# A stick-breaking attention stage: sigmoid(-z) goes into the PSUM bank of the scores instead of a ring in SBUF

## Chip, cores, metric

The kernel runs on one core of one Trainium2 chip. The metric is the device time of one execution in microseconds (us).

## The reference

One decoder layer over 1024 tokens of width 1024, all in float32: RMSNorm, one combined projection, a retention group (4 heads of 128), a stick-breaking attention group (8 heads of 64), an output projection, and a top-4-of-32 mixture of experts. The part that the change touches is the stick-breaking group. For each head and each block of 128 queries it computes

```python
z = einsum('bhqd,bhkd->bhqk', q_blk, kt) * scale
causal = key_pos[None, :] < q_pos[:, None]
log_one_minus = where(causal, log_sigmoid(-z), 0.0)
log_remaining = cumsum(log_one_minus, axis=3, reverse=True) - log_one_minus
weights = where(causal, exp(log_sigmoid(z) + log_remaining), 0.0)
out = einsum('bhqk,bhkd->bhqd', weights, vt)
```

So a weight is sigmoid(z) times the product of sigmoid(-z) over all later keys up to the query.

## The kernel before

The kernel is written out by hand for each engine, with semaphores between them; every engine runs its own list in program order. Its stages follow each other: norm and projections with the retention work (to about 403 us of the profiled execution), stick-breaking attention (403 to 566 us), output projection and routing (to about 715 us with the list work), and a loop over 32 experts from there to the end.

The attention stage works in *units*. A unit is one head, one block of 128 queries (i = 0 to 7) and up to 512 keys; a query block with more than 512 keys has two units per head, the later keys first. The two heads of a pair (par 0 and 1) always come together, so the work goes in doubles, units n and n+1 with n even. A pair has 24 units, the four pairs 96 (NU). In order, the 12 doubles of a pair have 128, 256, 384, 512, 128, 512, 256, 512, 384, 512, 512 and 512 columns (the fifth and sixth belong to i = 4, and so on). For a unit n:

- TensorE, scores(n) (L871 to L894, called with even n for both heads): three passes of matmuls of the split queries and keys into bank[n % 4] (L881, L884, L887), and for the block on the diagonal a matmul that adds a mask (L893). It raises z_ok.
- ScalarE, remains(n) (L681): sigmoid(-z) of the bank into `stick`, a ring of four units in SBUF. It raises z_not. sticks(n) (L688): sigmoid(z) of the same bank into `sig`, a ring of six in SBUF. It raises z_sig.
- VectorE, remaining(n) (L1256): a running product (tensor_tensor_scan, L1267) over stick[n % 4] from the last key to the first, into `rem`; its second input is a column of ones, broadcast. It raises z_rem. Where a query block has two units, the second starts from the first one's last value.
- GpSimd (L540 to L544): sig times rem, shifted by one, in place in sig. It raises z_w.
- TensorE, turn_weights(n) (L896): up to four 128x128 transposes into bank 4 or 5 (L901); ScalarE, turned(n) (L694): copy to `wgtT` (L699); TensorE, values(n) (L904): matmuls with the values into bank 6 or 7 (L913).

The order of the lists: TensorE runs values(n - 8), turn_weights(n - 4), turn_weights(n - 3), scores(n + 4) for n in steps of two. ScalarE runs turned(n - 6), turned(n - 5), remains(n), remains(n + 1), sticks(n), sticks(n + 1). VectorE runs remaining(n) for n in turn, and for a pair with another behind it four steps that split the next pair's queries and keys (pair_step, L1193: a cast L1198 or a subtraction L1201 over 1024 columns), behind units 6, 10, 14 and 18 of the pair's 24; a copy of a finished output bank (chain_out, L1273) comes ten units behind its last unit.

A score bank is used again four units later. scores(n) waits for the two sigmoids of unit n - 3 (z_not and z_sig at n - 2), and remains(n) waits for the running product of unit n - 4, since that read the same place of the ring. The stages behind start from z_pv (values of all units) and z_out.

Of the kernel before, what the change touches and what calls it, by code (L numbers as in the profile page):

```python
# [34 lines left out]
ACT = mybir.ActivationFunctionType  # L35
# [11 lines left out]
CH = 512  # L47
# [60 lines left out]
def layer(nc, x, attn_norm_g, w_in, ret_norm_g, sb_q_norm_g, sb_k_norm_g, w_out, ffn_norm_g,  # L108
          w_router, b_router, w_gate_up, b_gate_up, w_down, b_down, consts, rope, out):
    with ExitStack() as ctx:  # L110
# [3 lines left out]
        def sb(name, shape, dt=F32):  # L114
            return ctx.enter_context(nc.sbuf_tensor(name, shape, dt))

        def sem(name):
            return ctx.enter_context(nc.semaphore(name))
# [6 lines left out]
        ring = sb("ring", [P, 24576])  # L125
# [5 lines left out]
        bank = [ctx.enter_context(nc.psum_tensor(f"bank{i}", [P, 512], F32)) for i in range(8)]  # L131
# [17 lines left out]
        def region(t, at, *shape):  # L149
            n = int(np.prod(shape))  # L150
            v = t[:, at:at + n]
            if len(shape) == 1:
                return v
            names = "abcd"[:len(shape)]
            return v.rearrange(f"p ({' '.join(names)}) -> p {' '.join(names)}",
                               **{k: s for k, s in zip(names, shape)})
# [28 lines left out]
        prj_std = region(work, 9216, CH)  # L185
        rem = region(work, 0, 4, D + 2)
        wgtT = region(work, 4104, 4, CH)
        stick = region(ring, 3072, 4, CH)
        sig = region(ring, 5120, 6, CH)
        ident_r = region(ring_r, 128, P)  # L190
        mask_r = region(ring_r, 256, P)
# [77 lines left out]
        z_sig = sem("z_sig")  # L269
        z_not = sem("z_not")  # L270
        z_rem = sem("z_rem")
# [81 lines left out]
        units = []  # L353
        for p in range(SH // 2):
            for i in range(NT):
                for k0 in ((0,) if i < HT else (CH, 0)):
                    k1 = min(k0 + CH, (i + 1) * P)
                    for par in range(2):
                        units.append(dict(p=p, par=par, h=2 * p + par, i=i, k0=k0, n=(k1 - k0) // P, w=k1 - k0,
                                          at=D - (i + 1) * P + k0, row=(2 * (NT * p + i) + par) % 4,  # L360
# [18 lines left out]
        def unit_before(n):  # L379

            u = units[n]
            same = [m for m in range(n) if units[m]["row"] == u["row"] and units[m]["last"]]
            return same[-1] if same else None
# [212 lines left out]
        def _(e):  # L596
# [81 lines left out]
                            e.wait_ge(r_acc, c - 1)  # L678
                        e.activation(k_tok[:, c % 2], bank[4][:, :], ACT.Copy).then_inc(r_k, 1)

            def remains(n):  # L681
                w = units[n]["w"]
                e.wait_ge(z_ok, n + 1)
                if n >= 4:
                    e.wait_ge(z_rem, n - 3)
                e.activation(stick[:, n % 4, 0:w], bank[n % 4][:, 0:w], ACT.Sigmoid, scale=-1.0).then_inc(z_not, 1)  # L686

            def sticks(n):  # L688
                w = units[n]["w"]
                if n >= 6:  # L690
                    e.wait_ge(z_tr, n - 5)
                e.activation(sig[:, n % 6, 0:w], bank[n % 4][:, 0:w], ACT.Sigmoid).then_inc(z_sig, 1)

            def turned(n):  # L694
                w = units[n]["w"]
                e.wait_ge(z_tr, n + 1)
                if n >= 4:
                    e.wait_ge(z_pv, n - 3)
                e.activation(wgtT[:, n % 4, 0:w], bank[4 + n % 2][:, 0:w], ACT.Copy).then_inc(z_wT, 1)  # L699
# [3 lines left out]
            for n in range(0, NU + 6, 2):  # L703
                if n >= 6:
                    turned(n - 6)
                    turned(n - 5)
                if n < NU:
                    for m in (n, n + 1):
                        remains(m)
                    for m in (n, n + 1):  # L710
                        sticks(m)
            e.wait_ge(z_pv, NU)
            for i in range(2):
                e.dma_start(x_re[:, i], xr[i]).then_inc(xr_in[i], 16)
# [54 lines left out]
        def _(e):  # L769
# [101 lines left out]
            def scores(n):  # L871
                u = units[n]
                b, p = u["p"] % 2, u["p"]
                e.wait_ge(z_st, 4 * (p + 1))
                if n >= 4:
                    e.wait_ge(z_not, n - 2)
                    e.wait_ge(z_sig, n - 2)
                queries, keys = slice(u["i"] * P, (u["i"] + 1) * P), slice(u["k0"], u["k0"] + u["w"])
                heads = ((n, slice(0, HD)), (n + 1, slice(HD, P)))
                for m, pr in heads:  # L880
                    e.matmul(bank[m % 4][:, 0:u["w"]], q_hi[b][pr, queries], k_hi[b][pr, keys], start=True, stop=False,  # L881
                             skip_group_check=True)
                for m, pr in heads:
                    e.matmul(bank[m % 4][:, 0:u["w"]], q_hi[b][pr, queries], k_lo[pr, p, keys], start=False, stop=False,  # L884
                             skip_group_check=True)
                for m, pr in heads:
                    mm = e.matmul(bank[m % 4][:, 0:u["w"]], q_lo[pr, p, queries], k_hi[b][pr, keys], start=False,  # L887
                                  stop=not u["diag"], skip_group_check=True)
                    if not u["diag"]:
                        mm.then_inc(z_ok, 1)  # L890
                if u["diag"]:
                    for m, pr in heads:
                        e.matmul(bank[m % 4][:, u["w"] - P:u["w"]], ident_r, mask_r, start=False, stop=True,  # L893
                                 skip_group_check=True).then_inc(z_ok, 1)  # L894
# [28 lines left out]
            for n in range(-4, NU + 8, 2):  # L923
                if n >= 8:
                    values(n - 8)
                if 4 <= n < NU + 4:
                    turn_weights(n - 4)
                    turn_weights(n - 3)
                if n + 4 < NU:
                    scores(n + 4)  # L930
# [53 lines left out]
            for j in range(NT - 1):  # L984
                n = NT - 1 - j
# [124 lines left out]
        def _(e):  # L1110
# [92 lines left out]
            for g, u in enumerate(groups):  # L1203
# [34 lines left out]
                if c == 6:  # L1238
                    e.wait_ge(prj, g + 1)
                    at = SL * (u["slab"] % 2)  # L1240
# [15 lines left out]
            def remaining(n):  # L1256
                u = units[n]
                e.wait_ge(z_not, n + 1)
                if u["diag"]:
                    before_it = unit_before(n)  # L1260
                    if before_it is not None:
                        e.wait_ge(z_w, before_it + 1)
                    left = 1.0
                else:
                    e.wait_ge(z_rem, n - 1)
                    left = rem[:, u["row"], u["at"] + u["w"]:u["at"] + u["w"] + 1]
                e.tensor_tensor_scan(rem[:, u["row"], u["at"]:u["at"] + u["w"]][:, ::-1], stick[:, n % 4, 0:u["w"]][:, ::-1],  # L1267
                                     ones[:, 0:1].to_broadcast([P, u["w"]]), left, ALU.mult, ALU.mult).then_inc(z_rem, 1)

            def chain_out(n):  # L1270
# [7 lines left out]
            for n in range(NU + 10):  # L1278
                if n < NU:
                    remaining(n)  # L1280
                    p, j = n // PAIR + 1, n % PAIR - 6
                    if p < SH // 2 and 0 <= j < 16 and j % 4 == 0:
                        if j == 0 and p >= 2:
                            e.wait_ge(z_ok, PAIR * (p - 1))
                        pair_step(p, j // 4)
                if n >= 10 and units[n - 10]["ends"] and units[n - 10]["par"] == 1:
                    chain_out(n - 10)
# [248 lines left out]
```

## Time and profile before

| | |
|---|---|
| time, median of 3 runs | 2402.2 us (2400.37 to 2408.03) |
| the profiled execution's own time | 2400.01 us |
| its span in the profile | 2398.1 us |
| busy in the span | TensorE 95%, VectorE 41%, ScalarE 21%, GpSimd 15% |
| attention stage | 403 to 566 us |

The profile shows one execution. PE is TensorE (PEld its weight loads), DVE is VectorE, ACT ScalarE, POOL GpSimd; L1267 is line 1267 of the kernel. Busy time says how long an engine had an instruction in it, also while that instruction was held up. What a wait is put down to is the line that released it.

### The profile page before, as it was taken

How to read it: one execution, taken by the hardware profiler on the slowest of the kernel's cores; microseconds unless marked ns; L12 is line 12 of the kernel's file. 1: busy time of each engine (PE TensorE's matmuls, PEld its weight loads, DVE VectorE, ACT ScalarE, POOL GpSimd, SP SyncE). 2: the span in 40 equal slices, each digit the busy share in tenths (PEclk: the TensorE clock that was granted, in tenths of full speed). 3: DMA queues.
4: the chain of work that ended last, by engine and by line, in shares of the span. 5: the costliest groups of instructions: out<-in, count | busy, mean ns of one | idle time of the engine just before them, and what ended most of it. 6: DMA issues, size and time to landing. Idle time of an engine off the chain costs nothing.

```text
span 2398.1 us, 43829 instructions
## 1 busy us (share of the span) xinstructions
PE 2283.4 (95%) x17841; PEld 2167.5 (90%) x17842; DVE 994.9 (41%) x2198; ACT 492.9 (21%) x938; POOL 354.1 (15%) x263
## 2 busy tenths in 40 slices
PE   6999999888969999999999999999999999999997
PEld 5878888566869999999999999999999999999997
DVE  6435435997354333233333333332333333333332
ACT  4243144776111111011111111111111111111110
POOL 1101202894000100010010100010001010101001
PEclk9999999999969999999999999999999999999999
DMA  4222222003357888778888887887888887888882
GB/s 161 97 71 71 91 86 88 1 2 120 127 194 234 257 290 264 227 253 288 282 262 289 274 257 250 283 261 231 278 291 276 285 268 234 261 288 277 288 282 37
DMA packets 250237, 501.97 MB, mean 209 GB/s; under 512 B 7884, under 2 KB 36592, under 8 KB 250112
## 3 DMA queue, kind: packets, MB, share of 16 engines
q1 hardware_dynamic: 233888, 449.87, 53.7%
q0 software_dynamic: 14912, 45.71, 9.5%
q10 hardware_dynamic: 1344, 5.01, 0.7%
q8 instruction: 76, 1.25, 0.2%
q14 instruction: 17, 0.14, 0.0%
HBM read 469.46 MB, written 31.10 MB: 209 GB/s over the span
## 4 chain that ended last, share of the span: by engine, by line
PE 87%; issue 4%; DVE 3%; POOL 3%; ACT 1%; DMA 1%; DVEq 0%; ACTq 0%; POOLq 0%
PE bank L1045 43%; PE bank L1056 19%; PE bank L799 13%; POOL ring L544 3%; PE bank L1033 2%; DVE hx L1408 2%; PE bank L1004 2%; PE bank L948 1%; PE bank L950 1%; PE bank L949 1%; PE bank L996 1%; PE bank L901 1%; PE bank L807 1%; PE bank L913 0%; PE bank L969 0%
## 5 line engine op out<-in xcount | busy, mean ns | idle before, releaser
L1045 PE MATMUL bank<-hx,ring 128*128 128x140 f32 (+1 forms) x8192 | 1034.9, 288 | 25.3 <-issue 16.0
L1045 PEld LDWEIGHTS bank<-hx,ring 128*128 128x128 f32 x8192 | 1019.0, 197 | 32.3 <-issue 31.2
L1056 PE MATMUL bank<-hx,ring 128*128 128x140 f32 (+1 forms) x4096 | 514.7, 287 | 0.0
L1056 PEld LDWEIGHTS bank<-hx,ring 128*128 128x128 f32 x4096 | 507.0, 190 | 0.0
L755 ACT ACTIVATE hx<-hx 128x168 f32<-128x168 f32 x256 | 87.9, 343 | 1448.5 <-DVE hx L1479 1448.5
L1479 DVE TENSOR_SCALAR hx<-bank,hx 128x168 f32<-128x168 f32 x256 | 100.4, 392 | 638.7 <-PE bank L1045 638.5
L1504 DVE TENSOR_SCALAR hx<-bank,hx 128x168 f32<-128x168 f32 x256 | 100.5, 392 | 353.9 <-PE bank L1056 353.9
L569 POOL DMA_INDIRECT out_x<-mix,hx x66 | 99.7, 1511 | 817.0 <-ACT mix L748 774.7
L548 POOL DMA_INDIRECT mix<-xn_scratch,hx x66 | 64.9, 983 | 719.6 <-DVE hx L1403 709.5
L544 POOL TENSOR_TENSOR ring<-ring,work 128x512 f32<-128x512 f32 (+3 forms) x96 | 141.8, 1509 | 20.1 <-DVE work L1267 18.2
L799 PE MATMUL bank<-hx_r,mix_r 128*128 128x512 f32 x480 | 116.9, 403 | 8.5 <-DVE hx_r L1139 8.5
L799 PEld LDWEIGHTS bank<-hx_r,mix_r 128*128 128x128 f32 x480 | 92.7, 195 | 29.3 <-issue 9.8
L799 PE MATMUL bank<-hx_r,work_r 128*128 128x512 f32 x480 | 113.7, 394 | 0.0
L799 PEld LDWEIGHTS bank<-hx_r,work_r 128*128 128x128 f32 x480 | 89.7, 188 | 20.2 <-issue 1.9
L1485 DVE TENSOR_TENSOR hx<-hx 128x168 f32<-128x168 f32 x256 | 85.3, 333 | 50.9 <-ACT hx L755 50.9
L1481 DVE TENSOR_SCALAR hx<-bank,hx 128x168 f32<-128x168 f32 x256 | 98.1, 383 | 0.0
L1487 DVE SCALAR_TENSOR_TENSOR hx<-hx 128x168 f32<-128x168 f32 x256 | 85.2, 333 | 8.9
L1267 DVE TENSOR_TENSOR_SCAN work<-ring,cst 128x128 f32<-128x128 f32 (+3 forms) x64 | 83.3, 1349 | 2.3 <-ACT ring L686 2.2
L748 ACT ACTIVATE mix<-bank,hx 84x512 f32<-84x512 f32 x132 | 78.9, 674 | 19.1 <-PE bank L1033 19.1
L901 PE MATMUL bank<-cst,ring 128*128 128x128 f32 x288 | 51.5, 306 | 22.2 <-POOL ring L544 22.2
L901 PEld LDWEIGHTS bank<-cst,ring 128*128 128x128 f32 x288 | 33.3, 152 | 37.3 <-POOL ring L544 30.2
L1033 PE MATMUL bank<-cst,hx 128*84 128x128 f32 x528 | 63.1, 273 | 2.8 <-issue 2.8
(200 smaller groups left out, 1891.5 us busy)
## 6 DMA issues: line engine op xcount, KB each, us to landing
ring<-in_w_gate_up SPq DMA_DIRECT2D x128, 2048.0 KB, 11.0
ring<-in_w_down SPq DMA_DIRECT2D x64, 2048.0 KB, 8.7
mix<-in_w_in SPq DMA_DIRECT2D x14, 1024.0 KB, 5.0
work<-in_w_in SPq DMA_DIRECT2D x14, 1024.0 KB, 5.0
ring<-in_x SPq DMA_DIRECT2D x8, 512.0 KB, 8.0
hx<-in_w_out SPq DMA_DIRECT2D x1, 4096.0 KB, 12.8
work<-in_x ACTq DMA_DIRECT2D x8, 512.0 KB, 4.7
out_x<-work SPq DMA_DIRECT2D x8, 512.0 KB, 4.4
```

The costliest lines, as they stand in the source:

```text
L544: e.tensor_tensor(w, w, rem[:, u["row"], u["at"] + 1:u["at"] + 1 + u["w"]], ALU.mult).then_inc(z_w, 1)
L569: e.indirect_dma_start(out=out_rows, in_=yo[:, h], in_offset=None, compute_op=ALU.add, out_offset=bass.IndirectOffsetOnAxis(ap=idx_sc[:, h ...
L755: e.activation(sg[:, f % 2], g1[:, f % 2], ACT.Sigmoid, scale=GALPHA).then_inc(m_sig, 1)
L799: mm = e.matmul(dst, lhs, rhs, start=k == 0 and (xs is x_hi and ws is w_hi), stop=k == KD - 1 and ws is w_lo)
L901: mm = e.transpose(bank[4 + n % 2][:, t * P:(t + 1) * P], sig[:, n % 6, t * P:(t + 1) * P], ident)
L1033: mm = e.transpose(bank[4 + 2 * h + q][0:HC, r * P:(r + 1) * P], yT[:, 4 * q + r, h * HC:(h + 1) * HC], ident)
L1045: mm = e.matmul(bank[f % 2][:, part * CAP:part * CAP + w], gu_ring[:, k, f * 256 + part:(f + 1) * 256:2], xT[:, k, 0:w], start=k == 0, sto ...
L1056: return e.matmul(bank[2 + j % 2][:, 0:w], dn_ring[:, k, j * P:(j + 1) * P], hid[:, k, 0:w], start=k == 0, stop=k == KD - 1)
L1479: e.tensor_scalar(g1[:, b], bank[b][:, 0:CAP], be[:, f:f + 1], GLIM, ALU.add, ALU.min)\
L1481: e.tensor_scalar(u1[:, b], bank[b][:, CAP:2 * CAP], be[:, 8 + f:9 + f], GLIM + 1.0, ALU.add, ALU.min).then_inc(m_up, 1)
L1485: e.tensor_tensor(gs[:, b], g1[:, b], sg[:, b], ALU.mult).then_inc(m_gs, 1)
L1504: e.tensor_scalar(yT[:, j, :], bank[2 + j % 2][:, 0:CAP], be[:, 16 + j:17 + j], None, ALU.add)\
```

## The change

sigmoid(-z) is written over the scores in their own PSUM bank, and the running product reads it there. The ring `stick` goes. Since the scores are overwritten, sigmoid(z) has to be taken first: ScalarE's order within a double becomes sticks(n), remains(n), sticks(n + 1), remains(n + 1), and remains(n) waits for sticks(n) to complete (z_sig at n + 1). Since the bank is in use until the running product has read it, scores(n) now waits for z_rem at n - 2 in place of z_not and z_sig. remains no longer waits for z_rem.

```diff
-        stick = region(ring, 3072, 4, CH)
...
-            def remains(n):
+            def sticks(n):
                 w = units[n]["w"]
                 e.wait_ge(z_ok, n + 1)
-                if n >= 4:
-                    e.wait_ge(z_rem, n - 3)
-                e.activation(stick[:, n % 4, 0:w], bank[n % 4][:, 0:w], ACT.Sigmoid, scale=-1.0).then_inc(z_not, 1)
-
-            def sticks(n):
-                w = units[n]["w"]
                 if n >= 6:
                     e.wait_ge(z_tr, n - 5)
                 e.activation(sig[:, n % 6, 0:w], bank[n % 4][:, 0:w], ACT.Sigmoid).then_inc(z_sig, 1)
+
+            def remains(n):
+                w = units[n]["w"]
+                e.wait_ge(z_sig, n + 1)
+                e.activation(bank[n % 4][:, 0:w], bank[n % 4][:, 0:w], ACT.Sigmoid, scale=-1.0).then_inc(z_not, 1)
...
                     for m in (n, n + 1):
+                        sticks(m)
                         remains(m)
-                    for m in (n, n + 1):
-                        sticks(m)
...
                 if n >= 4:
-                    e.wait_ge(z_not, n - 2)
-                    e.wait_ge(z_sig, n - 2)
+                    e.wait_ge(z_rem, n - 2)
...
-                e.tensor_tensor_scan(rem[:, u["row"], u["at"]:u["at"] + u["w"]][:, ::-1], stick[:, n % 4, 0:u["w"]][:, ::-1],
+                e.tensor_tensor_scan(rem[:, u["row"], u["at"]:u["at"] + u["w"]][:, ::-1], bank[n % 4][:, 0:u["w"]][:, ::-1],
                                      ones[:, 0:1].to_broadcast([P, u["w"]]), left, ALU.mult, ALU.mult).then_inc(z_rem, 1)
```

## Rows read from the trace of the kernel before

**Rows 1.** The page's first part: busy us, share of the span, instructions.

```profile
PE 2283.4 (95%) x17841; PEld 2167.5 (90%) x17842; DVE 994.9 (41%) x2198; ACT 492.9 (21%) x938; POOL 354.1 (15%) x263
```

**Rows 2.** Busy time by stretch: PE, PEld, DVE, ACT, POOL, then PEclk, DMA, GB/s.

```profile
403.00:566.00 163.00, 138.03 (x1183) 97.68 (x1182) 158.24 (x118) 116.07 (x286) 141.92 (x100) 0.93 0.07 27
440.00:481.00 41.00, 34.27 (x307) 24.34 (x305) 40.98 (x31) 29.27 (x72) 35.14 (x25) 0.96 0.01 1
```

**Rows 3.** Waits in 403 to 566 us: total, times, longest.

```profile
PEld bank L901 <- POOL ring L544: 30.2, 35, 1.9
```

**Rows 4.** Single instructions in order of time: start, us; VectorE twice, GpSimd once.

```profile
499.63 1.27 DVE L1267 TENSOR_TENSOR_SCAN work<-ring,work,cst 128x512 f32<-128x512 f32 x1
440.54 2.05 DVE L1267 TENSOR_TENSOR_SCAN work<-ring,work,cst 128x512 f32<-128x512 f32 x1
439.50 2.01 POOL L544 TENSOR_TENSOR ring<-ring,work 128x512 f32<-128x512 f32 x1
```

**Rows 5.** VectorE's timeline at the pairs' boundaries and the end, merged.

```profile
485.61 8.48 DVE L1267 TENSOR_TENSOR_SCAN work<-ring,cst 128x128 f32<-128x128 f32 x7
...
526.55 12.88 DVE L1267 TENSOR_TENSOR_SCAN work<-ring,cst 128x128 f32<-128x128 f32 x10
...
559.81 4.18 DVE L1267 TENSOR_TENSOR_SCAN work<-ring,work,cst 128x512 f32<-128x512 f32 x2
```

**Rows 6.** Timeline of VectorE and GpSimd around 62 to 66 us.

```profile
62.30 2.28 DVE L1134 TENSOR_TENSOR work_r<-work,work_r 128x2048 fp32r<-128x2048 f32 x1
64.50 1.28 DVE L1128 TENSOR_TENSOR ring<-bank,small 128x512 f32<-128x512 f32 x2
...
62.46 3.27 POOL L529 TENSOR_TENSOR ring<-ring,work 128x512 f32<-128x512 f32 x1 [5.33 <-DVE ring L1223]
```

**Rows 7.** Timeline of TensorE and ScalarE, 485 to 496 us, merged.

```profile
485.48 0.44 PE L881 MATMUL bank<-ring_r 64*128 64x384 f32 x2
...
486.56 1.09 PE L913 MATMUL bank<-work,ring 128*64 128x128 f32 x16
...
487.59 1.09 PE L901 MATMUL bank<-cst,ring 128*128 128x128 f32 x8
488.28 1.09 ACT L699 ACTIVATE work<-bank 128x512 f32<-128x512 f32 x2 [0.99 <-PE bank L901]
488.61 0.49 PE L881 MATMUL bank<-ring_r 64*128 64x512 f32 x2
...
489.87 1.09 PE L913 MATMUL bank<-work,ring 128*64 128x128 f32 x16
...
491.59 1.09 ACT L686 ACTIVATE ring<-bank 128x512 f32<-128x512 f32 x2
...
493.78 0.22 PEld L881 LDWEIGHTS bank<-ring_r 64*128 64x128 f32 x2 [0.23 <-issue]
...
494.70 0.44 PE L913 MATMUL bank<-work,ring 128*64 128x128 f32 x4
...
495.07 0.88 PE L901 MATMUL bank<-cst,ring 128*128 128x128 f32 x6
```

**Rows 8.** ScalarE's timeline around 134 us: the second waits for the first.

```profile
134.05 0.69 ACT L649 ACTIVATE work<-bank,small 128x512 f32<-128x512 f32 x1 [0.26 <-PE bank L807]
134.77 0.63 ACT L651 ACTIVATE work<-work 128x512 f32<-128x512 f32 x1
```

**Rows 9.** Running products that start a query block: ns least, median, most.

```profile
L1267 DVE TENSOR_TENSOR_SCAN work<-ring,cst x64: 391/1410/2218, 405.5 to 557.7; 128x128 f32<-128x128 f32 x16, 128x256 f32<-128x256 f32 x16, 128x384 f32<-128x384 f32 x16, 128x512 f32<-128x512 f32 x16
```

**Rows 10.** The splitting steps on VectorE: ns least, median, most.

```profile
L1198 DVE CAST ring_r<-ring x8: 685/1151/1433, 385.1 to 507.7; 128x1024 fp32r<-128x1024 f32 x8
...
L1201 DVE TENSOR_TENSOR ring_r<-ring,ring_r x8: 1193/1316/1951, 386.1 to 515.3; 128x1024 fp32r<-128x1024 f32 x8
```

**Rows 11.** The chain in order of time where the stage starts, start and length.

```profile
403.96 0.15 DVE ring_r L1277
404.11 0.25 issue
```

## The prediction

> **What bounds the kernel now.** I began with the page. TensorE is busy for 95% of the span [rows 1], nearly all of it in stages that the diff does not touch: the projections before 403 us and the expert loop behind 715 us. I then cut out the stick-breaking stage, 403 to 566 us, and asked for the busy time of each engine in it. There VectorE is busy 158 of 163 us, and in a stretch of 41 us in the middle it is busy all 40.98 us, while TensorE has 34.3, GpSimd 35.1 and ScalarE 29.3 [rows 2]. So VectorE, with its running products (L1267), sets this stage. The list of waits agrees: TensorE's transposes wait 30.2 us for GpSimd's products (L544) [rows 3], which wait for the running products.
>
> The single instructions say why VectorE is full. A running product over 512 columns takes 1.27 us with GpSimd idle and 2.05 us with GpSimd in a product, whose own 512 columns then take 2.01 us [rows 4]. The two alternate: each stands while the other runs. One head pair (24 units) takes 40.94 us, from its first 128-column product at 485.61 to the next pair's at 526.55; the last pair, which has no splitting work for a next one, runs from 526.55 to 563.99 us, 37.4 us [rows 5].
>
> **What the change takes away.** The product's first operand comes from PSUM; of its SBUF inputs only the broadcast column of ones is left. Whether that ends the alternation is the first unknown cost. The nearest row is a VectorE multiply of a PSUM tensor by an SBUF one (L1128) that runs beside GpSimd's add (L529): two of them take 1.28 us from 64.50. The add, issued at 62.46, stood behind the subtraction L1134, which has two SBUF inputs and ends at 64.58; it ended at 65.73, so 1.15 us of it ran beside the two multiplies and neither was longer for it [rows 6]. Bounds: 1.27 us if the scan behaves like L1128, 2.05 us if it still takes turns. I take 1.27, because the form (PSUM and SBUF in) is that of L1128, plus 0.03 us for a PSUM source: L1128's single takes 0.68 us at 512 columns (its two take 1.28 with 0.08 of overlap), and the two-SBUF-input form takes 1.19 us at 1024 columns [rows 10], less 512 columns at the (2.28 - 1.19)/1024 us that L1134 [rows 6] gives, so 0.65.
>
> The Trainium skill ("SBUF — State Buffer", Who interferes with whom) has this as a rule: a DVE instruction with at most one SBUF input, outside the two-port modes, does not contend with GpSimd. By that rule the scan is free, and the trace agrees for L1128.
>
> VectorE's work for a pair is then, in full: 12 scans of 512 columns at 1.25, 4 each of 384, 256 and 128 at 0.96, 0.67 and 0.39 (a line through the shortest, 0.39 [rows 9], and 1.25), less 0.08 overlap each, 21 us; 3.4 us of splitting and 1.3 of copies: about 26 us. VectorE no longer bounds the stage.
>
> **What it adds on ScalarE.** The kernel had four sigmoids in a row that overlap: two of 512 columns take 1.09 us [rows 7], and each lasts 0.60 with 0.11 of overlap, as the copies do. Now each remains(n) waits for sticks(n) to complete, since it overwrites what that one reads. The row for a ScalarE instruction that waits for the one ahead of it is L651 behind L649: 134.05 + 0.69 = 134.74, start at 134.77 [rows 8], so 0.03 us between instead of 0.11 overlap: 0.14 us more each, 24 times. ScalarE's need becomes 29.3 + 24 x 0.14 = 32.6 us a pair. The write into PSUM has no row. The nearest: L651, which reads SBUF, takes 0.63 us [rows 8] and a sigmoid that reads PSUM 0.60, so the memory makes 0.03 on the reading side; I allow 0.05 off or on for the write and take nothing. The Trainium skill ("ScalarE: Activation LUTs", Step-by-step) says that a ScalarE write to PSUM is faster than one to SBUF; no run here shows it yet, and it would only shorten the sum. The sigmoid(-z) now comes behind sigmoid(z) of its unit, so the first scan of a double starts one sigmoid later.
>
> **What it adds on TensorE: the wait that decides.** scores(n) waited for two sigmoids; now it waits for the scan of unit n-3 (z_rem). With m for a double of two units (one for each head of the pair), TensorE's queue runs values(m-4), turn(m-2), scores(m+2), and scores(m+2) now starts at the end E(m) of m's second scan. Behind that stand values(m-3) and turn(m-1); ScalarE's queue holds its copies of turn(m-1) ahead of the sigmoids of double m+2; the second scan of m+2 ends the loop. So E(m+2) = E(m) + scores(m+2) + values(m-3) + turn(m-1) + copy + four sigmoids(m+2) + one scan + passing of semaphores. This is a ring of two doubles' length, all in program order, and no engine has to be full for it to bind.
>
> Its terms [rows 7]: from the start of scores to the start of the next work, 384 and 512 columns with the diagonal block take 1.08 and 1.26 us, 512 without it 0.92 (which I take for 256 with it too); values 1.03 us with 16 matmuls, 0.37 with 4; turn 1.02 us with 8 transposes; the smaller ones in between. From the first of 8 transposes to ScalarE's copy 0.69 us, and the two copies last 1.09, so they end 0.76 us behind the last transpose. Four sigmoids of 512 columns end 2.28 us behind the copy (four times 0.60 is 2.40; 0.03 is added at two places and about 0.09 taken off at two, where they still overlap). From VectorE's end to TensorE's start 0.15 us (0.25 at 404.11 [rows 11], where two operations are passed, and nearly nothing between other engines; I take between).
>
> A pair has 12 doubles: widths 128, 256, 384, 512, 128+512, 256+512, 384+512, 512+512. The ring couples each double to the second next, so odd and even doubles make separate chains. The odd one (256, 512, 512, 512, 512, 512) is the heavy one. Its six steps sum to: scores 5.9 + values 4.0 + turn 4.0 (these two are of even doubles) + copies 3.2 + sigmoids 12.9 + scans 7.6 (0.67 and five of 1.25, with 0.10 to 0.12 for PSUM, start and the first scan's overhang) + 0.9 of passing = 38.4 us. On top lies VectorE's splitting for the next pair: it is issued between the first and second scan of doubles 3, 5, 7 and 9, all odd ones, where the second scan is the one waited for. Undisturbed, a cast takes 0.69 and a subtraction 1.19 us [rows 10]; less 0.08 overlap each, 2 x (0.61 + 1.11) = 3.4 us. So 41.8 us a pair, where the alternation takes 40.94 today.
>
> TensorE alone would need 31.2 us a pair (scores 11.9, values 9.6, turn 9.7), ScalarE 32.6: both lie below the ring. What was gained at VectorE is spent on the trip round the ring.
>
> **The sum.** Three pairs with splitting +0.9 us each; the last 38.4 against 37.4, +1.0; the end of the stage loses one blocked GpSimd product, -0.8 (2.05 to 1.27). Together +2.9 us. The stages behind start from z_pv and z_out and keep their lengths, so it passes on in full. The profiled execution took 2400.0 us, 1.9 us around its span of 2398.1, and lies 2.2 us under the median of the three runs; 2402.2 + 2.9 = 2405.1, and I say 2405. A term that is off by 0.25 us in each of the 24 steps moves this by 6 us: the forecast's own range is 2396 to 2413. What a measurement can tell from no change is 0.3%, 7.2 us.
>
> **Rivals.**
> - The scan still takes turns with GpSimd (other side: slower). The place is L1267; the price is up to 0.8 us (2.05 against 1.27) on each of the 24 ring steps, 19 us: 2424. It decides from some 0.2 us a step. L1128 speaks against; that no scan with a PSUM operand is in the trace speaks for it.
> - The ring is longer than I say by its small parts (semaphores, a PSUM write that is slower by 0.05, a subtraction that GpSimd blocks to 1.95 [rows 10]): 0.4 us a step, 10 us more: 2415, slower.
> - The bank wait does not bind, because TensorE gets to scores after the scan anyway. Then ScalarE's 32.6 us sets the pair: 8.3 us less for three pairs and 4.8 for the last, about 30 us: 2372, and a half-way case (ring shorter by 0.6 us a step) 2390. For it: VectorE has 14 us of air a pair. Against: the sum, and scores(m+2) stands behind values and turn that themselves wait for ScalarE.
>
> **Chances.** Forecast 0.45 (most of it within 0.3%, a part beyond on the slow side), longer ring 0.22, turns with GpSimd 0.12, half-way 0.13, ScalarE alone 0.08. From them: faster by over 0.3% 0.21, within 0.42, slower 0.37. The range of 8 in 10 reaches from the half-way case to just past the turns, 2388 to 2426.
>
> **What would show it.** Right: scans of 512 columns near 1.3 us whether GpSimd runs or not; GpSimd's products near 1.3; VectorE's busy share in the stage down to some two thirds; TensorE at L881 waiting for L1267 (new in the list of waits), most behind doubles 3, 5, 7 and 9; a pair near 41.8 us and the last near 38.4. Wrong: scans at 2 us; L686's pieces shorter or longer than 0.6; no wait at L881, with ScalarE's copies (L699) never waiting, which would mean that ScalarE sets the pace and the time falls.

## The result, and the profile after

The changed kernel takes 2415.57 us (median of 4 runs, 2414.16 to 2417.26) against 2401.28 us: a ratio of 1.0058, 95% interval 1.0041 to 1.0075. It is slower, by 10 to 18 us. The forecast of 2405 us was 10.6 us too low: +2.9 us was forecast and +14.3 measured. The time lies in the stated range (2388 to 2426), on the side that had a chance of 0.37, and above the forecast's own range (2396 to 2413). The profiled execution took 2414.16 us, its span is 2412.3 us.

First the busy time by stretch in the changed kernel, in the columns of [rows 2]: the stage, then its second, third and last pair of heads.

```profile
403.00:578.00 175.00, 139.72 (x1206) 103.24 (x1206) 105.06 (x118) 124.70 (x288) 96.71 (x100) 0.90 0.07 25
...
449.50:490.20 40.70, 30.86 (x298) 22.79 (x296) 27.10 (x30) 31.06 (x73) 23.86 (x25) 1.00 0.00 1
490.20:534.40 44.20, 35.65 (x314) 26.50 (x316) 27.11 (x30) 31.24 (x73) 25.71 (x25) 0.92 0.01 1
...
534.42:575.02 40.60, 34.27 (x306) 25.48 (x307) 23.85 (x26) 30.63 (x71) 21.21 (x24) 0.92 0.00 1
```

No engine is full any more. VectorE, busy all the time before, has 24 to 27 us of work in a pair, GpSimd 21 to 26 instead of 35, and still a pair takes 40.6 to 44.2 us. The groups by line and form say what VectorE was relieved of (busy us, mean ns). First the kernel before, 403 to 566 us:

```profile
L544 POOL TENSOR_TENSOR ring<-ring,work 128x512 f32<-128x512 f32 x48 | 86.5, 1818 | 17.6 <-DVE work L1267 17.6
...
L1267 DVE TENSOR_TENSOR_SCAN work<-ring,work,cst 128x512 f32<-128x512 f32 x32 | 56.9, 1796 | 0.1
```

Then the changed one, 403 to 580 us:

```profile
L543 POOL TENSOR_TENSOR ring<-ring,work 128x512 f32<-128x512 f32 x48 | 64.5, 1344 | 49.6 <-DVE work L1263 48.9
...
L1263 DVE TENSOR_TENSOR_SCAN work<-bank,work,cst 128x512 f32<-128x512 f32 x32 | 40.2, 1275 | 29.2 <-ACT bank L690 28.9
...
L690 ACT ACTIVATE bank<-bank 128x512 f32<-128x512 f32 x48 | 27.9, 582 | 1.5
```

A running product (now L1263) takes 1.275 us in the mean over 32 instead of 1.796 (2.05 for one beside GpSimd [rows 4]), and none of 512 columns takes more than 1.28; GpSimd's products fell with it, from 1.82 to 1.34 us in the mean. And the waits in the stage, 403 to 580 us:

```profile
POOL ring L543 <- DVE work L1263: 73.5, 47, 4.8
DVE work L1263 <- ACT bank L690: 64.9, 38, 4.9
...
ACT work L697 <- PE bank L897: 42.4, 33, 3.6
PE bank L877 <- DVE work L1263: 32.7, 24, 2.9
```

In [rows 3] TensorE's transposes waited 30.2 us for GpSimd; of those waits 2.2 us are left. In their place each engine waits for the one ahead of it in the same circle: TensorE at scores (L877) for the running product, VectorE for the sigmoid (L690), ScalarE's copy (L697) for the transposes.

One step of the ring, in the third pair, from the timeline of all engines (start, length):

```profile
509.63 1.28 DVE L1263 TENSOR_TENSOR_SCAN work<-bank,work,cst 128x512 f32<-128x512 f32 x1
...
511.06 0.50 PE L877 MATMUL bank<-ring_r 64*128 64x512 f32 x2 [2.93 <-DVE work L1263]
...
511.95 0.88 PE L909 MATMUL bank<-work,ring 128*64 128x128 f32 x12
512.75 0.44 PE L897 MATMUL bank<-cst,ring 128*128 128x128 f32 x2
513.12 0.45 ACT L697 ACTIVATE work<-bank 128x128 f32<-128x128 f32 x2 [2.36 <-PE bank L897]
...
513.45 0.60 ACT L685 ACTIVATE ring<-bank 128x512 f32<-128x512 f32 x1
...
514.09 0.58 ACT L690 ACTIVATE bank<-bank 128x512 f32<-128x512 f32 x1
...
514.70 1.28 DVE L1263 TENSOR_TENSOR_SCAN work<-bank,work,cst 128x512 f32<-128x512 f32 x1 [2.63 <-ACT bank L690]
...
515.90 0.67 DVE L1194 CAST ring_r<-ring 128x1024 fp32r<-128x1024 f32 x1
...
516.49 1.28 DVE L1263 TENSOR_TENSOR_SCAN work<-bank,work,cst 128x512 f32<-128x512 f32 x1
```

The running product ends at 510.91. TensorE had waited 2.93 us for it and starts scores 0.15 us later, then values (511.95), transposes (512.75); ScalarE copies from 513.12 and takes the sigmoids from 513.45; the first running product starts at 514.70, the cast stands between it and the second, which ends at 517.77. That is 6.86 us for two doubles. The second sigmoid(-z) had ended at 515.79, so the cast alone made the second scan 0.6 us late.

Where did the 14.2 us between the two spans go? By the first 128-column running product of each pair, the pairs took 39.1, 41.0, 40.9 and 37.4 us before and 42.9, 40.7, 44.2 and 40.6 after (the last one up to the end of its last running product): 9.9 us. The stage began about 1 us later, and its end is 0.9 us shorter (from the last scan to the last output copy 4.4 instead of 5.3 us). The last copy starts 10.2 us later, at 579.43 against 569.26. The remaining 4 us lie in the expert loop, which took 1649.6 us before and 1653.8 after (first to last L1045, now L1041). The loop took 1648 to 1662 us in the profiles of all kernels here, and 1658.3 in one that differs from the one before only in ScalarE's order, so I do not count them as the change's.

**The granted clock.** The second pair ran with TensorE granted its upper level throughout (1.00) and took 40.70 us, a little less than the 40.96 of before. The third ran the same instructions and took 3.5 us more, at a mean grant of 0.92. In 6 us stretches:

```profile
516.00:522.00 6.00, 4.42 (x26) 2.62 (x23) 4.68 (x6) 5.07 (x11) 4.54 (x4) 0.80 0.00 0
522.00:528.00 6.00, 6.00 (x43) 4.65 (x44) 3.33 (x4) 3.09 (x7) 3.26 (x2) 0.64 0.01 3
```

TensorE's timeline there and, for comparison, one pair earlier:

```profile
487.89 1.09 PE L897 MATMUL bank<-cst,ring 128*128 128x128 f32 x8
...
524.05 1.97 PE L897 MATMUL bank<-cst,ring 128*128 128x128 f32 x8
```

Eight transposes take 1.97 us instead of 1.09: that is the lower of the two levels, 1.2 instead of 2.4 GHz. The kernel before has such a stretch in each pair but the last, too. What it costs there shows in a last pair that met it, that of the kernel before with another order of ScalarE's list (the control further down, 2399.60 us). First the last pair of the kernel before, at the upper clock, then that one:

```profile
526.55:563.99 37.44, 31.45 (x294) 22.00 (x296) 37.42 (x27) 28.71 (x69) 36.21 (x25) 1.00 0.01 2
...
524.70:562.19 37.49, 33.37 (x293) 23.40 (x291) 37.37 (x27) 28.85 (x68) 36.26 (x25) 0.91 0.01 2
```

TensorE's busy time is 1.9 us larger and the pair is as long. With splitting work it is the same: 41.14 us at 1.00 in the first experiment below, 40.96 and 40.94 at 0.96 in the kernel before. While VectorE was full, a slow TensorE was covered. On the ring it is not: in the changed kernel the third and the last pair are 3.3 and 3.2 us longer than before, at 0.92.

### The profile page after: what moved, and what is told of

The parts are those of the page before. It is cut to its first block, busy times and chain, and to the rows that moved or that the text cites. A ratio compares the mean times of both kernels' runs of the same rounds, so it can differ in the third digit from the quotient of the medians.

```text
span 2412.3 us, 43827 instructions
## 1 busy us (share of the span) xinstructions
PE 2284.5 (95%) x17841; PEld 2171.6 (90%) x17842; DVE 942.7 (39%) x2198; ACT 501.0 (21%) x938; POOL 306.9 (13%) x263
## 4 chain that ended last, share of the span: by engine, by line
PE 89%; DVE 5%; issue 4%; ACT 2%; DMA 1%; POOL 0%; DVEq 0%; ACTq 0%; POOLq 0%
PE bank L1041 42%; PE bank L1052 19%; PE bank L796 12%; PE bank L1029 2%; DVE hx L1404 2%; PE bank L1000 2%; PE bank L944 1%; PE bank L946 1%; PE bank L945 1%; PE bank L909 1%; PE bank L897 1%; DVE work L1263 1%; PE bank L992 1%; PE bank L877 1%; PE bank L804 1%
## 5 line engine op out<-in xcount | busy, mean ns | idle before, releaser
L1041 PE MATMUL bank<-hx,ring 128*128 128x140 f32 (+1 forms) x8192 | 1034.8, 288 | 28.1 <-issue 18.7
L1041 PEld LDWEIGHTS bank<-hx,ring 128*128 128x128 f32 x8192 | 1018.6, 197 | 35.2 <-issue 34.0
L543 POOL TENSOR_TENSOR ring<-ring,work 128x512 f32<-128x512 f32 (+3 forms) x96 | 96.5, 1015 | 74.9 <-DVE work L1263 73.5
L1263 DVE TENSOR_TENSOR_SCAN work<-bank,cst 128x128 f32<-128x128 f32 (+3 forms) x64 | 51.1, 818 | 36.6 <-ACT bank L690 36.0
L1029 PEld LDWEIGHTS bank<-cst,hx 128*84 128x84 f32 x528 | 59.7, 123 | 3.3 <-issue 2.9
L1404 DVE TENSOR_TENSOR hx<-bank,small 128x504 f32<-128x504 f32 (+1 forms) x99 | 55.4, 614 | 4.0 <-PE bank L1000 3.9
```

The lines of the kernel that those rows point to most:

```text
L543: e.tensor_tensor(w, w, rem[:, u["row"], u["at"] + 1:u["at"] + 1 + u["w"]], ALU.mult).then_inc(z_w, 1)
L1029: mm = e.transpose(bank[4 + 2 * h + q][0:HC, r * P:(r + 1) * P], yT[:, 4 * q + r, h * HC:(h + 1) * HC], ident)
L1041: mm = e.matmul(bank[f % 2][:, part * CAP:part * CAP + w], gu_ring[:, k, f * 256 + part:(f + 1) * 256:2], xT[:, k, 0:w], start=k == 0, sto ...
L1404: e.tensor_tensor(xT[:, 3 * m:3 * m + n, :], bank[4 + m][:, 0:n * CAP].rearrange("p (k t) -> p k t", t=CAP), g.unsqueeze(2).to_broadcast([ ...
```

## Experiments

The theory: scores(n) waits for the running product, and that closes a ring of TensorE, ScalarE and VectorE two doubles long; what lies on the ring costs, what does not is free. ("Ring" is from here on this closed loop of waits, not a buffer.) The rivals: ScalarE's longer chain (its own wait, the later sigmoid(-z)), running products that still take turns, and TensorE's clock.

### One part at a time, on the kernel before

**ScalarE's order and wait alone.** In remains(n) (sticks(n) takes over the wait for z_ok):

```diff
-                e.wait_ge(z_ok, n + 1)
+                e.wait_ge(z_sig, n + 1)
...
-                    for m in (n, n + 1):
-                        remains(m)
                     for m in (n, n + 1):
                         sticks(m)
+                        remains(m)
```

> The kernel before with ScalarE's part of the change alone: sticks(n), remains(n), sticks(n+1), remains(n+1), remains(n) waiting for sticks(n); sigmoid(-z) still goes to the ring in SBUF and scores wait for the two sigmoids. Ring theory (the wait of scores for the running product closes the loop): without that wait nothing binds but the running products that take turns with GpSimd, so 2401 us, within 3. Rival (ScalarE's longer chain, its own wait and the later sigmoid(-z), is the loss): as slow as the changed kernel, 2410 to 2416.

Measured: 2400.49 us, ratio 1.0003 (0.9992 to 1.0015). By itself ScalarE's part costs nothing that can be measured, in a kernel whose VectorE is full. Its profile still has the running products of 512 columns at a mean of 1.80 us. So this run says that ScalarE's part alone is not the loss; what it costs once the ring is closed it cannot say.

**The bank wait alone.**

```diff
-                    e.wait_ge(z_not, n - 2)
+                    e.wait_ge(z_rem, n - 2)
```

> The kernel before with the bank wait alone: scores(n) waits for the running product of unit n-3 (and the sigmoids), sigmoid(-z) still goes to SBUF, ScalarE's order is untouched, and the running product still has two SBUF inputs. Ring theory: the ring is there and its scans still take turns with GpSimd (up to 0.8 us on each of 24 steps), so slower than the changed kernel: 2415 to 2435. Rival (ScalarE's chain): 2401 us, like before.

Measured: 2424.68 us, ratio 1.0094 (1.0074 to 1.0114). This one line makes the kernel 23 us slower by the ratio (25 by the medians). A running product from VectorE's timeline shows that with two SBUF inputs it still takes turns with GpSimd:

```profile
471.85 2.11 DVE L1267 TENSOR_TENSOR_SCAN work<-ring,work,cst 128x512 f32<-128x512 f32 x1
```

How much of the 23 us is the ring's length and how much the clock, this run does not separate. In its profile, that of its slowest execution, only the last pair is at the upper clock:

```profile
547.02:586.64 39.62, 32.40 (x317) 23.97 (x318) 32.00 (x26) 29.28 (x73) 30.51 (x24) 1.00 0.01 2
```

That is 2.2 us more than the 37.44 of before. The other three are 6.2, 6.4 and 7.4 us longer, at 0.81 to 0.86 and with the splitting steps on the ring.

So the change is two things of opposite sign: its wait costs some 23 us, and the rest of it gives about 9 of them back (2424.7 to 2415.6). The rest is the operand's move to PSUM together with ScalarE's order; no run here takes these two apart on the ring.

### Taking things off the ring, in the changed kernel

**The sigmoids ahead of the copies in ScalarE's list.** Same instructions, other order.

```diff
             for n in range(0, NU + 6, 2):
-                if n >= 6:
-                    turned(n - 6)
-                    turned(n - 5)
                 if n < NU:
                     for m in (n, n + 1):
                         sticks(m)
                         remains(m)
+                if n >= 6:
+                    turned(n - 6)
+                    turned(n - 5)
```

> The changed kernel with ScalarE's list turned round within a step: the four sigmoids of n and n+1 first, then the two copies of n-6 and n-5. Ring theory: values, turn and copies (about 12 us of 38 in a pair) fall out of the loop that goes through the scores' banks; what is left is under ScalarE's own 32.6 us a pair, so a pair takes 33 to 37 us and the time is 2385 to 2400 us. Rival (ScalarE's work or VectorE's waits for it set the pace): the work is the same, so 2412 to 2418 us.

Measured: 2397.29 us, ratio 0.9992 (0.9982 to 1.0001), 18 us less than the changed kernel by the medians and 16 by the ratios, from an order alone; the rival (2412 to 2418) is out. A pair with splitting work takes 39.37 us, at the upper clock throughout:

```profile
444.06:483.43 39.37, 32.20 (x308) 23.42 (x306) 26.78 (x31) 31.42 (x73) 24.52 (x25) 1.00 0.00 1
```

and over the whole stage TensorE's wait for the running product fell from 32.7 to 12.7 us, while a wait of the transposes for ScalarE's copies came in:

```profile
PE bank L897 <- ACT work L697: 13.6, 21, 1.5
PE bank L877 <- DVE work L1263: 12.7, 15, 1.2
```

My 33 to 37 us for a pair was too good: the new loop is through the copies.

Nor are the 16 to 18 us the length of the ring alone. The four pairs of this profile are 14.5 us shorter than those of the changed kernel (153.9 against 168.4). The second pair, at 1.00 in both, gives only 1.3 of them (39.37 against 40.70). The third and the last, at 1.00 here and at 0.92 there, give 4.9 and 3.3, the first, at 0.82 here and 0.76 there, 5.0. So most of what the order gives comes together with TensorE being at its upper level for longer. It also waits less; that the clock stayed up for that reason is not shown.

**The splitting steps behind the second running product** (instead of between the two of a double).

```diff
-                    p, j = n // PAIR + 1, n % PAIR - 6
+                    p, j = n // PAIR + 1, n % PAIR - 7
```

> The changed kernel with the four splitting steps of a pair one unit later, behind the second running product of a double and not between the two. Ring theory: they leave the loop (0.6 and 1.1 us, twice a pair, three pairs), so up to 10 us less than the changed kernel: 2405 to 2409 us; the waits of TensorE for the running product get shorter by as much. Rival (VectorE has air, its work is hidden wherever it stands; or the lower TensorE clock makes the loss): 2414 to 2417 us.

Measured: 2405.71 us, ratio 1.0031 (1.0017 to 1.0045), 10 us less than the changed kernel by the medians, 6.5 by the ratios: in the range of the ring theory, and the rival (2414 to 2417) is out. TensorE's waits for the running product fell from 32.7 to 25.2 us in its profile. Its third pair, at 0.92 like the changed kernel's, took 42.57 us against 44.21; the last, which has no splitting, 40.42 against 40.59. VectorE is idle for 14 us of every pair, and still it matters where in its list 3.4 us a pair stand.

**Both.**

> The changed kernel with ScalarE's sigmoids ahead of its copies and the splitting steps behind the second running product. Ring theory: with the sigmoids first the way round the scores' banks no longer bounds (a pair measured 39.4 us, its TensorE waits went to ScalarE's copies), and another loop is next: copies(m-3), turn(m-2), scores(m+2), sigmoids, copies. The splitting steps still delay a scan by 1 us twice a pair; out of the way they give up to 3 us a pair: 2388 to 2396 us. Rival (their place is only felt while the bank wait bounds): 2396 to 2399 us, as with the sigmoids first alone.

> The version with both edits once more, with more rounds, against the kernel before and beside the changed kernel on the same chip: 2390 to 2396 us, clear of both.

Measured: 2393.18 us, ratio 0.9971 (0.9960 to 0.9982), and again 2392.56 us, ratio 0.9970 (0.9959 to 0.9981), beside the changed kernel's 2413.58. This beats the kernel before by 4 to 10 us and the changed one by some 21. Both times lie in the range of the ring theory; the rival (2396 to 2399) is out. One pair of it, 1.6 us shorter than with the sigmoids first alone at the same clock:

```profile
441.25:478.98 37.73, 32.41 (x308) 23.45 (x306) 26.79 (x31) 31.43 (x73) 24.72 (x25) 1.00 0.00 1
```

**Copies and sigmoids interleaved**, with the splitting steps moved:

```diff
             for n in range(0, NU + 6, 2):
-                if n >= 6:
-                    turned(n - 6)
-                    turned(n - 5)
-                if n < NU:
-                    for m in (n, n + 1):
+                for m in (n, n + 1):
+                    if n < NU:
                         sticks(m)
                         remains(m)
+                    if n >= 6:
+                        turned(m - 6)
```

> The changed kernel with ScalarE's list interleaved, sticks(n), remains(n), turned(n-6), sticks(n+1), remains(n+1), turned(n-5), and the splitting steps behind the second running product. A copy now comes half a step earlier, so TensorE's next transposes wait less, and one copy more lies in the loop of the scores' banks. Ring theory: between the two orders or better than both, 2385 to 2396 us. Rival (ScalarE's total sets the pace): the same as with the sigmoids first and the splitting moved, within 2 us.

Measured: 2393.67 us, ratio 0.9977 (0.9967 to 0.9987): within 0.5 us of the version with both edits (2393.18), as the rival said; the range of the ring theory holds it too, so it does not decide.

**Sigmoids first in the kernel before**, as a control:

```diff
-                if n >= 6:
-                    turned(n - 6)
-                    turned(n - 5)
                 if n < NU:
                     for m in (n, n + 1):
                         remains(m)
                     for m in (n, n + 1):
                         sticks(m)
+                if n >= 6:
+                    turned(n - 6)
+                    turned(n - 5)
```

> The kernel before, with sigmoids ahead of copies and nothing else. It separates what the order gives by itself from what it gives in the changed kernel. Ring theory: before, VectorE and GpSimd take turns the whole time and no order of ScalarE's list shortens that, so 2398 to 2403 us. Rival (the order is worth some 18 us in any kernel): 2382 us.

Measured: 2399.60 us, ratio 1.0001 (0.9991 to 1.0010). The order is worth 16 us or more in the changed kernel and nothing in this one, where no ring is closed and VectorE is full.

**remains(n) and remains(n+1) behind both sticks**, in the changed kernel:

```diff
                     for m in (n, n + 1):
                         sticks(m)
+                    for m in (n, n + 1):
                         remains(m)
```

> The changed kernel with ScalarE's four sigmoids as sticks(n), sticks(n+1), remains(n), remains(n+1). remains(n) no longer waits for the instruction right ahead of it (0.14 us each saved, 24 a pair), but the first running product starts about half a microsecond later and the second stands behind it. Ring theory: only the end of the second running product counts; it comes 0.2 to 0.4 us later on each of 24 steps, so 5 to 9 us more than the changed kernel: 2420 to 2425 us. Rival (ScalarE's stalls are what the change costs): 3.4 us a pair less, near 2403 us.

Measured: 2414.28 us, ratio 1.0050 (1.0031 to 1.0069), with the changed kernel at 2413.58 on the same chip. Both expectations missed. Four sigmoids and their overlaps end some 0.3 us earlier (2.06 us instead of 2.33 for 512 columns), and the first running product starts later. By the medians the two about cancel, though with four runs between 2408.90 and 2423.85 us a few us either way stay open; its last pair took 41.75 us at 0.92, against 40.59 and 40.60 in two profiles of the changed kernel at the same grant. What it rules out is that ScalarE's stalls are the loss.

### TensorE's clock

**Zero matmuls ahead of the wait in every other double.** `zeros` is 128x64 in the place of the old ring, set once by GpSimd; the product is added to an output bank that is open, so the result stays what it was.

```diff
+            def fill(n):
+                u = units[n]
+                if n // 2 % 2 == 0 or units[n + 1]["ends"]:
+                    return
+                for _ in range(8):
+                    e.matmul(out_bank(u)[0:HD, u["i"] % HT * P:(u["i"] % HT + 1) * P], zeros, ident,
+                             start=False, stop=False, skip_group_check=True)
...
+                if n >= 8 and n + 4 < NU:
+                    fill(n - 8)
                 if n + 4 < NU:
                     scores(n + 4)
```

> The changed kernel with eight small matmuls of zeros (added to an open output sum, so nothing in the result changes) that TensorE does ahead of its wait for the running product in every other double. Clock theory: the parts of the stage at the lower granted clock follow stretches in which TensorE waited, and since TensorE now lies on the loop they cost some 3 us in three of the four pairs; with the wait filled the clock stays at the upper level, a pair takes near 41 us, and the time falls to 2403 to 2410 us. Rival (the clock stretches are no part of the loss): TensorE does more in the loop, so 2415 to 2420 us.

Measured: 2415.91 us, ratio 1.0068 (1.0052 to 1.0085), in the range of the rival. It does not decide: a fill took 2.0 us, and the four of the second pair stand ahead of scores for which TensorE waited 0.3, 0, 2.9 and 1.9 us in the changed kernel, so most of them lengthened the ring; pairs of 45.4 us at 0.96 and 46.9 at 0.93 in the profile mix both.

**Only in the long waits, and shorter than they are.** Where no output is open, the zeros go to the bank of the next one, before it starts.

```diff
-                if n // 2 % 2 == 0 or units[n + 1]["ends"]:
-                    return
-                for _ in range(8):
+                m = n // 2 + 6
+                times = ({5: 2, 7: 5, 9: 2} if m >= 36 else {1: 4, 5: 4, 7: 10, 9: 5}).get(m % 12, 0)
...
+                for _ in range(times):
```

> The changed kernel with the zero matmuls again, now only ahead of those scores for which TensorE's waits for the running product were 1 us or more in the first trace, and shorter than those waits (2 to 10 matmuls of 0.24 us, fewer in the last pair), so that they do not lengthen the loop. Clock theory: with the waits filled the lower clock comes less often, the pairs keep near 41 us, and the time is 2403 to 2410 us. Rival: the clock falls as before, or a pair is as long at the upper clock, so 2412 to 2418 us.

Measured: 2419.31 us, ratio 1.0076 (1.0060 to 1.0093), outside both ranges. As a remedy it failed: two pairs still met the lower clock and took 44.2 us each. Its last pair did not, and it gives the price once more. Busy time in that pair, against 40.60 us at 0.92 in the changed kernel:

```profile
536.26:573.70 37.44, 33.46 (x324) 24.92 (x321) 23.86 (x26) 30.57 (x71) 21.01 (x23) 1.00 0.01 2
```

Its expert loop took 1661.6 us, 8 us more than the changed kernel's; why, and how much of the median that is, I cannot say.

**The changed kernel once more.**

> The changed kernel once more in the same call: 2412 to 2418 us. If the lower clock stretches are part of the loss, its second profile shows pairs without one near 40.7 us and pairs with one 2 to 4 us longer.

Measured: 2413.58 us, ratio 1.0053 (1.0037 to 1.0069). The clock part of the expectation can be read only on the side of the loss, since no pair ran at the upper level throughout, and there one pair lost more than the 2 to 4 us that I gave it. The second and third pair of its profile:

```profile
448.06:495.64 47.58, 39.03 (x308) 29.00 (x310) 27.10 (x31) 31.22 (x73) 24.94 (x25) 0.82 0.00 1
495.64:540.10 44.46, 35.88 (x306) 26.48 (x305) 27.11 (x30) 31.16 (x73) 24.50 (x24) 0.88 0.01 1
```

The second pair took 40.70 us at 1.00 in the first profile and 47.58 at 0.82 here, 6.9 us more. VectorE's, ScalarE's and GpSimd's busy times are the same within 1.1 us; TensorE's is 8.2 us larger.

## Why the prediction was right or wrong

**What bounds the kernel: right.** VectorE's alternation with GpSimd set the stage, and it ended: 1.28 us for a running product that reads PSUM (forecast 1.30), also beside GpSimd's products (one of 1.28 us stands at 516.49, where a product runs from 516.07 to 517.53), which themselves took 1.34 in the mean instead of 1.82. The rule of the Trainium skill ("SBUF — State Buffer", Who interferes with whom) held for this instruction as for L1128. The rival that the turns go on is out; a kernel that has them inside the ring is the one with the bank wait alone.

**The wait that decides: right.** The ring exists, shown from both sides: the wait alone makes the kernel before slower by 23 us, and taking the copies or the splitting steps off the ring gives 16 to 18 and 6 to 10 us in the changed kernel, where the first gives nothing in the kernel before. At equal clock the amounts are smaller: 2.2 us for the wait in a pair without splitting, 1.3 for the copies and 1.6 for the splitting steps in a pair with it. TensorE waited at scores (L877) for the running product, as forecast, most behind doubles 3, 5, 7 and 9 (1.1, 2.9, 1.6 and 1.9 us in the second pair, from 449 to 490 us).

**Its terms: right in kind, a little too large.** From VectorE's end to TensorE's start 0.15 us (forecast 0.15); a sigmoid behind its own wait 0.04 us later (0.03); a sigmoid(-z) written into PSUM 0.58 us against 0.60 in the mean before (taken as no difference). At the upper clock a pair took 40.70 us where I had 41.8, the last pair 37.44 where I had 38.4. The splitting steps were undisturbed, 0.67 and 1.20 us, as forecast. The six terms of the prediction add up to 38.5, not 38.4 us, which changes nothing. The Trainium skill ("ScalarE: Activation LUTs", Step-by-step) says that a ScalarE write to PSUM is faster than one to SBUF; the trace agrees, by 0.02 us.

**The sum: wrong, by a term that is not in it.** I wrote "Three pairs with splitting +0.9 us each; the last 38.4 against 37.4" with every TensorE row taken from a stretch at the upper clock. The row of [rows 2] said 0.96 for 41 us in the middle, and each such pair of before had TensorE at its lower level for a while; it cost nothing (37.49 us at 0.91 against 37.44 at 1.00) because VectorE covered it. That cover went with the change, and the step should have asked what it hid. Measured: at the upper clock the pairs come out at -0.3 us (second) and 0.0 (last, in the kernel with fillers); with the lower clock +3.3 and +3.2 us in the first profile, +6.6 and +3.5 for the second and third pair in the other. The first pair is 3.8 us longer; there too TensorE is at the lower level for longer, but the start of the stage is in it, and the two are not separated. So in the two pairs that ran at the upper clock the ring costs nothing against before, less than forecast; the loss is in the pairs that met the lower clock.

**The rivals.** "The ring is longer by its small parts" named 2415 us and its time came true, but not its cause, so that match is luck: the small parts came out shorter than forecast. ScalarE alone as the bound never came: in the fastest kernel it is busy 31.4 of 37.7 us. That ScalarE's part costs something by itself is refuted for the kernel before; on the ring only its stalls were tested, and taking them out gained nothing.

**What is open.** TensorE's grant fell after stretches in which it had waited: in the changed kernel it was busy 3.18 us of the six from 420, ahead of the fall near 426 us, and 4.42 of the six from 516, in which another fall lies. But similar stretches came without a fall (3.94 of 6 from 456), and filling the waits did not prevent it. That pairs of the same list are 3 to 7 us longer with the lower clock on the ring is shown; what brings it on is not. Nor is it proved that it is the whole of the difference between 2405 and 2415.6 us: the two profiles of the changed kernel end the attention stage 10.2 and 15.8 us later than the one before, and the expert loop differs by up to 14 us between profiles for reasons that stay open.

## What to carry to other kernels

When a buffer moves to where its consumer reads it, look at whose reuse wait moves with it: here the full engine was relieved by a third, and the time rose, because a bank was now held until the last reader had gone, an order that had been harmless put three engines on one ring, and nothing covered TensorE's lower clock any more. Add up that ring in program order, not only the busy time of each engine; then take off it whatever may stand elsewhere (16 to 18 and 6 to 10 us here from reordering alone, a good part of the first together with more time at TensorE's upper clock). And when the engine that covered others is relieved, price what it covered, a lower TensorE clock too.

## What the runs showed of the hardware that I had not expected

A running product with one input in PSUM and one in SBUF (1.28 us at 512 columns) is untouched by GpSimd, while the form with both in SBUF takes 2.05 to 2.11 us beside it: the operand's place is worth 0.8 us for such an instruction, 0.5 in the mean over 32. The same list of instructions for a pair took 40.70 us at a grant of 1.00 and 47.58 at 0.82 in two executions, while the busy times of VectorE, ScalarE and GpSimd stayed within 1.1 us. Where VectorE was full, a pair took 37.44 us at 1.00 and 37.49 at 0.91.
